# Routing of a two-tile MoE block: per-tile logits, picks, positions and gather, with the row split shared by three engines

## The reference

```python
h = h + merged @ w_out[layer]
h = h + hierarchical_moe(rmsnorm(h, norm_ffn_w[layer]), router_group_w[layer], ...)
out = rmsnorm(h, norm_final_w)
return out[:, N_META:]

def hierarchical_moe(u, w_grp, b_grp, w_rtr, b_rtr, w_gate, w_up, w_down):
    grp_probs = jax.nn.softmax((xt @ w_grp + b_grp), axis=-1)
    p_grp, g_idx = lax.top_k(grp_probs, 1)                       # one of 4 groups
    exp_logits = (xt @ w_rtr + b_rtr).reshape(-1, N_EXPERT_GROUPS, EXPERTS_PER_GROUP)
    sel_logits = jnp.take_along_axis(exp_logits, g_idx[:, :, None], axis=1)[:, 0]
    w_e, e_idx = lax.top_k(jax.nn.softmax(sel_logits, axis=-1), TOP_K_IN_GROUP)   # two of its 8 experts
    w_e = w_e / jnp.sum(w_e, axis=-1, keepdims=True)
    ...
    for gi in range(N_EXPERT_GROUPS):
        hdn = silu(einsum('nd,edf->nef', xt, w_gate[gi])) * einsum('nd,edf->nef', xt, w_up[gi])
        hdn = hdn * comb[:, gi, :, None]
        y = y + jnp.einsum('nef,efd->nd', hdn, w_down[gi])
    return y
```

## Time and profile before

| | us |
|---|---|
| median of 3 runs (lowest to highest) | 797.16 (796.98 to 799.54) |
| profiled execution, its own time | 797.85 |
| its span in the trace | 796.1 |
| busy in the span: TensorE / VectorE / ScalarE / GpSimd | 768.1 / 313.5 / 309.4 / 103.6 |
| share of DMA in the span | 79% |

### The profile page before, as it was taken

One profiled execution on the slowest core, in us unless ns is written; L12 is line 12 of the kernel. 1 busy time (PEld: TensorE's weight loads), 2 busy tenths in 40 slices (PEclk: granted clock), 3 DMA queues, 4 the chain that ended last, 5 costly groups with the idle time before them and its releaser, 6 DMA issues.

```text
span 796.1 us, 15899 instructions
## 1 busy us (share of the span) xinstructions
PE 768.1 (96%) x6477; PEld 541.0 (68%) x6477; DVE 313.5 (39%) x781; ACT 309.4 (39%) x615; POOL 103.6 (13%) x153
## 2 busy tenths in 40 slices
PE   7998999999999999999999999999999999999895
PEld 6998999999999986565555555555555555555352
DVE  4587588777676741451122111211211121111112
ACT  6676576866776761311111212121212121121123
POOL 4154230322550232000000000000000000000000
PEclk7997999999999999999999999999999999999998
DMA  7545266465565338999999999999999999999992
GB/s 160 155 122 147 62 157 147 127 172 135 134 159 148 88 103 295 390 368 428 429 426 427 426 428 428 425 429 427 428 425 428 427 426 427 427 427 428 425 411 88
DMA packets 79951, 241.05 MB, mean 303 GB/s; under 512 B 6785, under 2 KB 65266, under 8 KB 67330
## 3 DMA queue, kind: packets, MB, share of 16 engines
q1 hardware_dynamic: 79570, 239.19, 78.7%
q10 hardware_dynamic: 304, 0.79, 0.4%
HBM read 238.92 MB, written 1.05 MB: 301 GB/s over the span
## 4 chain that ended last, share of the span: by engine, by line
PE 84%; DMA 5%; issue 4%; DVE 3%; SPq 1%; ACT 1%; DVEq 0%
PE banks L1982 25%; PE banks L1687 21%; PE banks L2036 13%; DMA ring<-in_expert_w_up_dram 5%; PE banks L1921 4%; PE banks L1859 3%; PE banks L1993 3%; PE banks L2014 1%; PE banks L1785 1%; PE banks L1798 1%; PE banks L1846 1%; PE banks L1802 1%; PE banks L1823 1%; PE banks L1789 1%; DVE desk L1277 1%
## 5 line engine op out<-in xcount | busy, mean ns | idle before, releaser
L1982 PE MATMUL banks<-ring,bench 128*64 128x256 f32 x2048 | 241.9, 389 | 6.5 <-DMA ring<-in_expert_w_up_dram 3.0
L1982 PEld LDWEIGHTS banks<-ring,bench 128*64 128x64 f32 x2048 | 149.9, 134 | 104.6 <-issue 28.4
L1687 PE MATMUL banks<-rounded 128*128 128x272 f32 (+2 forms) x1368 | 203.3, 298 | 2.1 <-DVE rounded L1239 2.0
L1687 PEld LDWEIGHTS banks<-rounded 128*128 128x128 f32 (+1 forms) x1368 | 177.2, 191 | 8.2 <-DVE rounded L1239 2.5
L1586 DVE TENSOR_TENSOR bench<-banks,bench 128x256 f32<-128x256 f32 x32 | 13.6, 424 | 263.7 <-PE banks L1982 150.2
L2036 PE MATMUL banks<-ring,bench 128*64 128x512 f32 x504 | 115.2, 599 | 1.5 <-ACT bench L1002 1.5
L1013 ACT ACTIVATE ysb<-banks 64x512 f32<-64x512 f32 x63 | 37.3, 592 | 121.5 <-PE banks L2036 120.7
L1002 ACT ACTIVATE bench<-banks 128x256 f32<-128x256 f32 x32 | 12.3, 385 | 172.7 <-PE banks L2014 172.7
L2036 PEld LDWEIGHTS banks<-ring,bench 128*64 128x64 f32 x504 | 33.4, 136 | 60.8 <-issue 53.6
L803 ACT ACTIVATE rounded<-room 128x1024 fp32r<-128x1024 f32 x56 | 58.9, 1051 | 15.0 <-PE banks L1687 14.9
L1226 DVE TENSOR_TENSOR rounded<-room,rounded 128x1024 fp32r<-128x1024 f32 x45 | 57.3, 1274 | 17.2 <-ACT rounded L803 16.1
(11 more groups left out here) (276 smaller groups left out, 833.6 us busy)
## 6 DMA issues: line engine op xcount, KB each, us to landing
ring<-in_expert_w_gate_dram SPq DMA_DIRECT2D x31, 2048.0 KB, 26.0
ring<-in_expert_w_up_dram SPq DMA_DIRECT2D x30, 2048.0 KB, 26.2
ring<-in_expert_w_down_dram SPq DMA_DIRECT2D x30, 2048.0 KB, 25.8
room<-in_w_in_dram SPq DMA_DIRECT2D x56, 512.0 KB, 4.2
ring<-in_w_out_dram SPq DMA_DIRECT2D x8, 512.0 KB, 3.6
ring<-in_expert_w_gate_dram SPq DMA_DIRECT2D x4, 512.0 KB, 6.3
ring<-in_expert_w_up_dram SPq DMA_DIRECT2D x4, 512.0 KB, 6.4
ring<-in_expert_w_down_dram SPq DMA_DIRECT2D x4, 512.0 KB, 6.3
```

The costliest lines, as they stand in the source:

```text
L1687: ins = T.matmul(o, a, b[:, k, lo_at:L], start=(k == 0 and n == 0), stop=(k == KT - 1 and n == 2))
L1982: ins = T.matmul(pb[5 + c][half * 64:half * 64 + SLOTS, 0:256], xgT[:, q % ROOMS, kt, j * SLOTS:(j + 1) * SLOTS], w[:, kt, half], start=(k ...
```

## The change

- The router's logits go to bank 7 for tile 0 and to bank 6 for tile 1, and `logits` is raised for each tile. The transposes of tile 1 alternate between two banks instead of three. ScalarE takes 11 of the 16 casts (before: 7), VectorE 5 (before: 9). The root of the mean is taken for each tile.
- VectorE picks for tile 0, finds its slots and makes its half of `hot`; then the same for tile 1. `before` now includes the token itself, so adding one is left out. The indices are compared without being cast first.
- TensorE's `place(i)` finds the positions of one tile. The counts for `most` (`count_all`) come behind expert 0's gate, and `down` of expert 0 waits for `most`.
- The first gather goes by tile and half: three parts of tile 0, then tile 1, and the fourth part last.
- GpSimd makes `xhi` and `xlo` of tile 0 in three passes (multiply, multiply in place, subtract); ScalarE makes `xhi` and VectorE `xlo` of tile 1.
- VectorE brings parts 0 and 2 of quad 0, ScalarE parts 1 and 3 (semaphore `xgT_side`).
- ScalarE copies `xres` to `kept` (in the room of `x2T`), and the four residual products (`seed`) come behind the up products of experts 0 and 1.

```diff
-CAST_ACT = [0, 1, 2, 3, 4, 14, 15]
+CAST_ACT = [0, 1, 2, 3, 4, 10, 11, 12, 13, 14, 15]
+SEEDS_AT = {0: [0, 1], 1: [2, 3]}
+FIRST_BANK = [5, 4, 7, 6]
...
+kept = merged[:].rearrange("p k t -> p (k t)")
+def turn_bank(n):
+    return 4 + (n % 3 if n < KT else n % 2)
...
-                sp.wait_ge(S("logits"), 1)
+                sp.wait_ge(S("logits"), TT)
...
+    def power(i):
         act.wait_ge(S("summed"), 2 * i + 2)
         if i:
             act.wait_ge(S("ms"), 3 + i)
         nc.scalar.activation(junk2, xn[:, i, :], ACT.Square, scale=1.0 / 32.0, accum_out=rs[:, i, 0:1]).then_inc(S("ms"), 1)
-        if i == 0:
-            for n in CAST_ACT:
-                if n < KT:
-                    cast(n)
-    act.wait_ge(S("ms"), 3 + TT)
-    nc.scalar.activation(rs[:, :, 22:23], rs[:, :, 0:1], ACT.Sqrt, bias=eps[:]).then_inc(S("rms"), 1)
+    def root_mean(i):
+        act.wait_ge(S("ms"), 3 + i + 1)
+        nc.scalar.activation(rs[:, i, 22:23], rs[:, i, 0:1], ACT.Sqrt, bias=eps[:]).then_inc(S("rms"), 1)
+    power(0)
+    root_mean(0)
+    for n in CAST_ACT:
+        if n < KT:
+            cast(n)
+    power(1)
     for n in CAST_ACT:
         if n >= KT:
             cast(n)
-    act.wait_ge(S("rinv"), 1)
+    root_mean(1)
+    act.wait_ge(S("rinv"), TT)
+    nc.scalar.activation(xhi[:, 1, :], xn[:, 1, :], ACT.Copy, scale=rs[:, 1, 1:2]).then_inc(S("xhi"), 1)
+    act.wait_ge(S("logits"), TT)
     for i in range(TT):
-        nc.scalar.activation(xhi[:, i, :], xn[:, i, :], ACT.Copy, scale=rs[:, i, 1:2]).then_inc(S("xhi"), 1)
+        nc.scalar.activation(kept[:, i * D:(i + 1) * D], xres[:, i, :], ACT.Copy).then_inc(S("kept"), 1)
...
+    act.wait_ge(S("kept"), TT)
+    for part in (1, 3):
+        act.wait_ge(S("gathered"), part + 1)
+        for k in (2 * part, 2 * part + 1):
+            nc.scalar.activation(xgT[:, 0, k, :], pb[FIRST_BANK[part]][:, (k - 2 * part) * WIDE:(k - 2 * part + 1) * WIDE], ACT.Copy,
+                                 scale=gain[:, k:k + 1]).then_inc(S("xgT_side"), 1)
...
-    chain(nc.gpsimd.affine_select(out=below[:], in_=ones[:], compare_op=ALU.is_gt, fill=0.0, base=0,
+    chain(nc.gpsimd.affine_select(out=below[:], in_=ones[:], compare_op=ALU.is_ge, fill=0.0, base=0,
...
+    pool.wait_ge(S("rinv"), 1)
+    nc.gpsimd.tensor_scalar(xhi[:, 0, :], xn[:, 0, :], rs[:, 0, 1:2], None, ALU.mult).then_inc(S("x_first"), 1)
+    pool.wait_ge(S("x_first"), 1)
+    pool.wait_ge(S("turned"), 2 * KT)
+    chain(nc.gpsimd.tensor_scalar(xn[:, 0, :], xn[:, 0, :], rs[:, 0, 1:2], None, ALU.mult))
+    nc.gpsimd.tensor_tensor(xlo[:, 0, :], xn[:, 0, :], xhi[:, 0, :].bitcast(F32), ALU.subtract).then_inc(S("x_first"), 1)
...
     dve.wait_ge(S("gain_land"), 16)
...
+    def inverse_rms(i):
+        dve.wait_ge(S("rms"), 4 + i)
+        V.reciprocal(rs[:, i, 1:2], rs[:, i, 22:23]).then_inc(S("rinv"), 1)
+        dve.wait_ge(S("rinv"), i + 1)
+    inverse_rms(0)
+    chain(V.memset(rt[:, :, 1, 0:8], NEG))
...
-    def both(f):
-        for i in range(TT):
+    def pick(i):
...
+        dve.wait_ge(S("logits"), i + 1)
+        chain(V.scalar_tensor_tensor(rt[:, i, 0:2, :].rearrange("p a c -> p (a c)")[:, 0:36], pb[7 - i][:, 0:36],
+                                     rs[:, i, 1:2], rbias[:], ALU.mult, ALU.add))
+        chain(V.max(row(2)[:, 0:8], row(1)[:, 0:8]))
+        chain(V.max_index(ru[:, i, 0:8], row(2)[:, 0:8], row(1)[:, 0:8]))
+        chain(V.tensor_tensor(row(3), iota_g[:], ru[:, i, 0:1].to_broadcast([P, EXPERTS]), ALU.not_equal))
+        chain(V.scalar_tensor_tensor(row(4), row(3), NEG, row(0), ALU.mult, ALU.add))
+        chain(V.max(row(5)[:, 0:8], row(4)))
+        chain(V.max_index(ru[:, i, 8:16], row(5)[:, 0:8], row(4)))
+        for k in range(2):
             counts["dve_chain"] += 1
...
+            V.tensor_tensor(row(6 + k), iota_e[:], ru[:, i, 8 + k:9 + k].to_broadcast([P, EXPERTS]), ALU.is_equal).then_inc(S("dve_chain"), 1)
         dve.wait_ge(S("dve_chain"), counts["dve_chain"])
...
-    V.tensor_tensor(ticks, row(6), row(7), ALU.add).then_inc(S("picked"), 1)
...
-    V.scalar_tensor_tensor(plan[:, :, 0:TT].rearrange("p e t -> p t e"), pb[7][:, 128:192].rearrange("p (t e) -> p t e", t=TT), 1.0, ticks.bitcast(F32),
-                           ALU.add, ALU.mult).then_inc(S("plan"), 1)
...
+        V.tensor_tensor(ticks[:, i, :], row(6), row(7), ALU.add).then_inc(S("picked"), 1)
+        dve.wait_ge(S("picked"), i + 1)
+    def first_slots(i):
+        dve.wait_ge(S("pos"), i + 1)
+        V.tensor_tensor(plan[:, :, i], pb[4 + 2 * i][:, 64 * i:64 * i + EXPERTS], ticks[:, i, :].bitcast(F32), ALU.mult).then_inc(S("plan"), 1)
+        dve.wait_ge(S("plan"), i + 1)
+        V.tensor_tensor(hot[:, i, :].rearrange("p (g s) -> p g s", g=4), iota_c[:].rearrange("p (o s) -> p o s", o=1).to_broadcast([P, 4, SLOTS]),
+                        plan[:, 0:4, i:i + 1].to_broadcast([P, 4, SLOTS]), ALU.is_equal).then_inc(S("hot"), 1)
+    pick(0)
+    first_slots(0)
+    inverse_rms(1)
+    pick(1)
+    first_slots(1)
...
     def settle():
         dve.wait_ge(S("total"), 1)
-        chain(V.max(most[:], pb[5][:, 192:224]))
+        chain(V.max(most[:], pb[7][:, 0:EXPERTS]))
         V.tensor_copy(mosti[:], most[:, 0:1]).then_inc(S("most"), 1)
-        for i in range(TT):
-            dve.wait_ge(S("xhi"), i + 1)
-            dve.wait_ge(S("turned"), KT + KT * (i + 1))
-            V.scalar_tensor_tensor(xlo[:, i, :], xn[:, i, :], rs[:, i, 1:2], xhi[:, i, :].bitcast(F32), ALU.mult, ALU.subtract).then_inc(S("xlo"), 1)
-        weigh()
...
         again = not isinstance(ps, int)
...
-        slots_of(0)
-        if not again:
+        if again:
+            slots_of(0)
+            for part in range(PARTS):
+                bring(0, part)
+        else:
+            dve.wait_ge(S("xhi"), 1)
+            V.scalar_tensor_tensor(xlo[:, 1, :], xn[:, 1, :], rs[:, 1, 1:2], xhi[:, 1, :].bitcast(F32), ALU.mult, ALU.subtract).then_inc(S("xlo"), 1)
+            weigh()
+            dve.wait_ge(S("kept"), TT)
+            bring(0, 0)
+            bring(0, 2)
+            weighed()
             settle()
-        for part in range(PARTS):
-            bring(0, part)
-        if not again:
-            weighed()
...
-    for n in range(TT * KT):
-        if n >= 3:
-            cast_off(n - 3)
-        k, i = n % KT, n // KT
-        pe.wait_ge(S("summed"), 2 * i + 2)
-        T.transpose(pb[4 + n % 3][:, 0:P], xn[:, i, k * P:(k + 1) * P], ident[:]).then_inc(S("turned"), 1)
-        if n >= 3:
-            logit(n - 3)
-    for n in range(TT * KT - 3, TT * KT):
-        cast_off(n)
-        logit(n)
-    for i in range(TT):
-        for half in range(2):
-            T.matmul(pb[2 * i + half], ident[:], xres[:, i, half * 512:(half + 1) * 512], start=False, stop=True, skip_group_check=True)
-    pe.wait_ge(S("picked"), 1)
+    def behind(n):
+        return n - 3 if n < KT else n - 2
+    for n in range(TT * KT + 2):
+        made = range(max(behind(n - 1) + 1, 0), behind(n) + 1)
+        for m in made:
+            cast_off(m)
+        if n < TT * KT:
+            k, i = n % KT, n // KT
+            pe.wait_ge(S("summed"), 2 * i + 2)
+            T.transpose(pb[turn_bank(n)][:, 0:P], xn[:, i, k * P:(k + 1) * P], ident[:]).then_inc(S("turned"), 1)
+        for m in made:
+            logit(m)
     pe.wait_ge(S("rconst"), 1)
-    T.matmul(pb[7][:, 128:160], before, ticks[:, 0, :], start=True, stop=True)
-    T.matmul(pb[7][:, 160:192], every, ticks[:, 0, :], start=True, stop=False)
-    T.matmul(pb[7][:, 160:192], before, ticks[:, 1, :], start=False, stop=True).then_inc(S("pos"), 1)
-    T.matmul(pb[5][:, 192:224], every, ticks[:, 0, :], start=True, stop=False)
-    T.matmul(pb[5][:, 192:224], every, ticks[:, 1, :], start=False, stop=True).then_inc(S("total"), 1)
+    def place(i):
+        pe.wait_ge(S("picked"), i + 1)
+        where = pb[4 + 2 * i][:, 64 * i:64 * i + EXPERTS]
+        if i:
+            T.matmul(where, every, ticks[:, 0, :], start=True, stop=False)
+        T.matmul(where, before, ticks[:, i, :], start=(i == 0), stop=True).then_inc(S("pos"), 1)
+    def count_all():
+        T.matmul(pb[7][:, 0:EXPERTS], every, ticks[:, 0, :], start=True, stop=False)
+        T.matmul(pb[7][:, 0:EXPERTS], every, ticks[:, 1, :], start=False, stop=True).then_inc(S("total"), 1)
+    def seed(n):
+        i = n // 2
+        pe.wait_ge(S("kept"), i + 1)
+        T.matmul(pb[n], ident[:], kept[:, n * 512:(n + 1) * 512], start=False, stop=True, skip_group_check=True)
+    place(0)
...
         def gather_first():
-            pe.wait_ge(S("hot"), 1)
             per = KT // PARTS
-            pe.wait_ge(S("xhi"), TT)
             def products(x, part, t):
...
-            for part in range(PARTS):
-                if part == 1:
-                    pe.wait_ge(S("most"), 1)
-                for t in range(TT):
-                    products(xhi, part, t)
+            pe.wait_ge(S("hot"), 1)
```

(35 more changed lines are left out.)

62 lines of the change are left out of this document (20 added, 42 removed).

## The result

| | before | after |
|---|---|---|
| median of 6 runs each, us (lowest to highest) | 797.44 (796.36 to 799.54) | 801.84 (801.28 to 803.64) |
| profiled execution, its own time | 797.85 | 802.63 |
| its span in the trace | 796.1 | 800.9 |

The changed kernel is slower: the ratio is 1.0056, with a 95% interval of 1.0040 to 1.0071, that is 4.4 us by the medians and 4.8 us by the two profiled executions. The prediction said 799.1 and within 0.3%; the time lies inside its range, and outside its own case's range of 797.5 to 801. More than 0.3% slower had a chance of 0.36 there.

The account below looks back on a forecast made before the run. Bound: a fixed-length DMA weight stream with one routing-set hole, at most 2.7 us to gain. Terms -2.15 + 1.8 + 1.4 + 0.85 = +1.9 us gave 799.1 us on the median's scale, range 795.4 to 802.2.

Parts of the forecast that it names:

- own case: The prediction's main case, all four terms together: 799.1 us, its own range 797.5 to 801; chance 0.45.
- The bound: Expert stage is a fixed-length DMA stream; routing sets its one hole, so a shorter routing gains at most 2.7 us.
- Term 1: Routing by tile: shorter chains of picks, `hot` and gather start the first gate product 2.15 us earlier.
- Term 2: GpSimd's subtraction holds a small two-input VectorE operation in picks of tile 1: +1.8 us, bounds 0 and 2.3.
- rival D: GpSimd's scalar passes block VectorE's picks too: gate at about 347, +4.7 us, 801.9; chance 0.11.
- Term 3: TensorE's clock falls while idle between 338 and 341.5, slowing some 14 of the gather's products: +1.4 us.
- rival C's smaller case: Lower clock lasts through the gather and a third of the gate: +3.5 us, 800.7; chance of C 0.12.
- Term 4: Residual and count products delay release of expert 0's down slot by 1.85 us, less 1.0 margin: +0.85 us.
- covered by the 0.85 already paid: Expert 1's down, 3.15 us margin against 3.5 of delay, was claimed to cost nothing more.
- the margin at expert 0's down: Stream reaches expert 0's down at 359.7, its issue is good for 358.7, so 1.0 us was to spare.
- issue-to-stream time: Time from SyncE's issue to the hole's effective end, taken as 1.5 us from expert 3's gate load.

Follow-up runs that it names:

- e4: Changed kernel with the four residual products back in TensorE's wait for the picks, without ScalarE's copies to `kept`: +2.1 us, ratio 1.0023 against the kernel before.
- e3: Changed kernel with GpSimd's subtraction replaced by a one-input pass that writes zeros: +2.8 us, ratio 1.0032 against the kernel before.
- e2: Changed kernel with 12 idle products on TensorE behind the positions of tile 0: +4.4 us, ratio 1.0054 against the kernel before.
- e1: Changed kernel without its four residual products (result lacks the residual): +4.3 us, ratio 1.0047 against the kernel before.
- e11: Changed kernel with twelve idle products behind the first position product and without the residual products: +2.5 us, ratio 1.0009 against the kernel before.
- e7: Kernel before with two idle 128x512 products behind the up products of experts 0 and 1: +1.1 us, ratio 1.0016 against the kernel before.
- e8: Kernel before with 22 of the first gate products repeated, so the gate issue comes later: +4.8 us, ratio 1.0070 against the kernel before.
- e9: Kernel before with both the idle products of e7 and the repeated gate products of e8: +7.1 us, ratio 1.0076 against the kernel before.
- e12: Changed kernel with only the count products moved from behind expert 0's gate to behind expert 1's up: +4.5 us, ratio 1.0052 against the kernel before.
- e5: Changed kernel with GpSimd keeping only its first pass and VectorE making both low halves, residual products unmoved: +2.7 us, ratio 1.0026 against the kernel before.

## Why the prediction was right and wrong, point by point

The direction of the sum was right, its size was not: 1.9 us were expected and 4.4 came. By the down issue, the four terms as measured are -1.82 + 2.84 + 1.80 + 2.04 = +4.86; the last of them is a delay, and its price was lower.

**The bound.** It held. The stage is a DMA stream of fixed rate, the hole is at its start, and nothing in the routing matters but when the freed slots are issued. In the changed kernel the issues from expert 1's down to 675 us have a lag of 6.4 us and the last one 4.83: a queue stands ahead of them, so that the median gate load of this kernel lands 23.6 us after its issue (26.0 before). What the 6.4 us cost is the dip near 388 us, and no more of it is to be seen.

**Term 1, the shorter chains: -2.15 predicted, about -1.8 measured.** In e4 the clock stays up and the collisions are there; its gate issue has a lag of 1.02, and 1.02 - 2.84 = -1.82, where 2.84 is term 2 as measured below. (So this is a remainder, and it holds also what e4's residual products and its missing copies on ScalarE change.) The picks of tile 0, less what the collision adds, took 2.28 us where 2.25 were predicted.

**Term 2, GpSimd beside VectorE: +1.8 predicted, +2.8 measured, and elsewhere.** The mechanism was right and the place wrong. A scalar pass of 1024 took 2.84 us and not 3.2, so the subtraction came at 336.05, ahead of the picks of tile 1, and met `hot` of tile 0, itself made late by the other hold; it held it for 2.55 - 0.43 = 2.12 us. The other 0.72 us (0.91 against 0.19 in the masking of tile 0) came with the start of the second scalar pass, at 333.11. I had used, where an operation ran across such a pass unheld, to say that scalar passes never block; rival D said that they always do. Both are wrong: in this kernel the pass held an operation with two SBUF inputs only at its start, until 1.17 us after it (333.37 + 0.91 - 333.11) and 1.32 us after it in e3. Even there it is not all: the group mask at 333.12, within 0.01 us of the pass's start, took 0.22 us against 0.19 for tile 1, and the operation of the earlier trace rows began 0.49 us into a shorter pass (128x256) and was not held. What decides it stays open. The Trainium skill, "SBUF — State Buffer", section "Who interferes with whom", has VectorE's two-input instructions contend with any GpSimd instruction that reads SBUF. By that rule, the traces agree for the subtraction (336.12 to 338.67 beside 336.05 to 338.39), and for a scalar pass only in its first 1.2 to 1.3 us.

**Term 3, the clock: +1.4 predicted, +1.4 to +1.8 measured.** The fall came earlier and the return far later than I said: it fell within 336 to 337 after TensorE had done nothing from 335.76 on, and stayed at the lower level through nearly the whole gather, to within 346 to 347. That is the course of rival C's smaller case, but the clock was back just ahead of the gate product (347.18), which ran at the upper level. The gate's issue is 1.43 us sooner in e2, with its late first gather, and 1.80 us in e4, which both hold the clock. The size is luck in part: I had counted 14 products at the lower level, and all 32 of the gather lay there; at 0.10 us each that would be 3.2 us, but TensorE also waited for VectorE in between (0.72 us ahead of 341.10).

**Term 4, the moved products: +0.85 predicted, some +1.2 to +1.8 measured.** The delay of the down issue was sized well: 1.56 us for two residual products (1.7 predicted) and 0.48 for the count products (0.2), 2.04 together. Its price was put too low. Four pairs of kernels differ by the residual products alone (after and e1, e2 and e11, before and e7, e8 and e9): 0.9 to 1.2 us of stream, and 1.0, 1.3 and 1.3 us in the last issue where e2 is left out; the medians scatter from 0.1 to 2.3. The count products are worth 0.2 us in the last issue and 0.5 of stream (e12). Two steps were wrong. Expert 1's down was not "covered by the 0.85 already paid": the dip from 384 to 392 us costs some 0.4 us more. And the margin at expert 0's down was a little smaller than 1.0 us: in e7 a delay of 1.57 us costs 0.7 us of stream by then, which leaves 0.9. I had taken the issue-to-stream time as 1.5 us from the *loss* in the hole, where a burst that comes early makes up for a gap that follows; until the full rate it was 2.4 to 3.0 us.

**The sum.** The gate was 1.8 us later than predicted (2.82 against 1.05): 0.3 by term 1, 1.0 by term 2 and 0.4 by term 3. The slots cost 0.4 to 1.0 us more than predicted. Together that is 2.2 to 2.8 us, against the 2.5 between 1.9 and 4.4; the step that failed most is term 2, by its place and size, and then term 4. That the time lies inside the range is owed to rival D, whose 801.9 us and gate "at about 347" it meets almost exactly. That is luck: by D the first pass would have held the picks of tile 0 until 333.4, and it was over at 333.01 before their first step with two SBUF inputs (333.12), the second held 0.72 us, and part of the rest is term 4.

**What stays open.** The low rate from 356 to 366 us in the changed kernel (382 GB/s, about 1 us of stream) has no cause here: without the residual products it is still 375 (e1), and with the late gate alone 429 (e8). e1 and e2 lie about 1 us above the down rule, inside their intervals, e2 by 1.9 us in its last issue. In e2 the bytes do not show that: 3.3 us of stream are missing, but expert 3's down matrix, issued at 360.86, takes 11.9 us to land, 6.4 us later than before by the cast, and most loads behind it land some 5.3 us late to the end. Something delays the end of each load by 2 us more than its bytes. That the DMA engines get out of step with each other in such a restart would fit, but it was not tried. Why the dip near 388 us comes some 12 us behind the late issue is open too.

## What to carry to other kernels

Where one matrix stream bounds a stage, ask for each freed slot when the queue ahead of it runs out, and look at the stream in windows of half a microsecond at a place where it restarts; the loss in a hole is not a lead time. Work moved "into the slack" of a busy engine lengthens the next release by its whole duration, and two or three releases behind a hole there is little slack: 1.57 us in each of two slots cost 0.9 to 1.3 us. Add up the bytes of a stretch and compare them with the kernel before; that told runs apart that the times did not. Before a second engine is given a pass over SBUF, look at which two-input operations of VectorE stand beside it, and try the variant in which VectorE does the work in its own waits: here that one, with the residual products back in TensorE's idle time, was the only one which lost nothing.

## What the runs showed of the hardware

- A GpSimd pass with one tensor input (128x1024 fp32, 2.84 us) held a VectorE operation with two SBUF inputs that began 0.07 to 0.26 us into it until 1.2 to 1.3 us into it; such operations later in the pass took their usual time, and one that began with it 0.22 us instead of 0.19. It did so in every run that had the second pass: 0.91 us against 0.19.
- From the issue of a 2048 KB load into a queue that was empty or running out to the full rate took 2.4 to 3.0 us, in a burst (some 0.5 to 1 us long), a gap of 0.5 to 1 us at a low rate, and only then the stream.
- TensorE's granted clock stayed at the lower of its two levels (1.2 GHz) for 10 us in the changed kernel, through nearly the whole gather, and for 6 us in e5, where the wait ahead of the fall was 0.84 us. Four residual products (e4) or twelve idle ones (e2, e11) in the wait kept it at 2.4 GHz.
